# Delta-net stage: a head's four input projections as two pairs of seven half-size products

## The chip, the cores and the metric

The kernel runs on one core of one Trainium2 chip. The core has a matrix engine (TensorE, PE in the profile, with its weight loads as PEld), a vector engine (VectorE, DVE), a scalar engine (ScalarE, ACT), a general engine (GpSimd, POOL), and DMA queues, here issued by SyncE (SPq) and ScalarE (ACTq). They run side by side and wait for each other by semaphores. The metric is the device time of one execution in microseconds (us).

## The reference

Two blocks of a residual network on a 512 x 1024 activation, all float32. The change touches one mixer of the first block, a gated delta-net with 8 heads of width 128:

```python
proj = h @ w_in
qkv, z, a, bt = jnp.split(proj, [n_qkv, n_qkv + H * dv, n_qkv + H * dv + H], axis=-1)
qkv = jax.nn.silu(causal_dwconv(qkv, conv_w))          # 4 taps along the sequence
q, k, v = jnp.split(qkv, [H * dk, 2 * H * dk], axis=-1)
q = _l2norm(_chunk_heads(q, H, C)) * (dk ** -0.5)
k = _l2norm(_chunk_heads(k, H, C))
...                                                     # beta, g, decays from a and bt
sol = lax.linalg.triangular_solve(kk + eye, rhs, left_side=True, lower=True, unit_diagonal=True)
u, w = sol[..., :dv], sol[..., dv:]
...                                                     # a scan over chunks makes o
o = o * lax.rsqrt(jnp.mean(o * o, axis=-1, keepdims=True) + 1e-6) * norm_w
o = o * jax.nn.silu(z)                                  # gate
return o.reshape(b_, s, H * dv) @ w_out
```

Per head there are four projections of the same input h (512 x 1024): q, k, v and z, each by 1024 x 128 weights.

## The kernel before

Everything is kept transposed: `HT` (128 x 8 x 512) holds the input, features on partitions. The weights come through `ring`, three slots of 2 MB; one slot holds a head's four units q, k, v, z (128 x 8 x 128 each). Between the heads' loads stand those of `ada` (weights of a conditioning vector), which VectorE sums in place (`dve_ada`, L387); a slot's next load is issued when its last reader is done.

A unit is 8 matmuls of 128 x 128 weights against 512 columns into one bank (`pe_dense4`, L1264). In float32 every matmul is two records in the trace. VectorE reads the bank with four convolution taps (`dve_conv4`: L1622 the first, L1625 three more), ScalarE applies SiLU (`silu`, L1522); the fourth unit, z, goes through `gate` (L1550) to the one buffer `zs`.

A head is an iteration h of a loop with two parts. First six levels of a blockwise triangular inverse. In each level TensorE makes `LD` (L1396), VectorE masks it (`Tm`, L1747), TensorE makes `TE` (L1414), VectorE subtracts (`inv`, L1753), TensorE transposes (`DT`, L1422), VectorE copies (`D`, L1768), and the next `LD` waits for that. Between these TensorE fills in the projections of head h+1: `fill` places 2, 1 and 1 matmuls behind LD, TE and DT. Then comes the scan over four chunks (L1434 to L1460), with 8 matmuls of head h+2 (`ahead`) between its steps, and the start of the next head's chain on VectorE: `lower` (L1683), `d_first` (L1696, L1699), `e_first` (L1704, L1706), the end of `dve_ada`, `gated` (L1717), `inner` (L1712). GpSimd has three products per head: two masks (`decay`, L1829 and L1832) and the scaled query (`qe`, L1838). All orders are written out by hand; each engine runs its list in order.

`khat` (L1671) and `qhat` (L1676) scale key and query, `kk` (L1318) is the first product of the next head. The final head fills with matmuls of the output projection (`gdn_ahead`) instead. The feed-forward stages (`pe_up`, L537) already use seven products of half size, with 256 columns each.

## Time and profile before

| | us |
|---|---|
| median of 3 runs | 2706.67 |
| lowest and highest | 2705.37, 2707.93 |
| the profiled execution's own time | 2705.38 |
| its span from first to last instruction | 2703.6 |

Between the span and the profiled execution's time lie 1.8 us outside the instructions. The delta-net stage reaches from about 43 us to about 520 us of the span.

### The profile page before, as it was taken

What the parts mean: (1) busy time and instruction counts of PE and PEld (TensorE: products, weight loads), DVE (VectorE), ACT (ScalarE), POOL (GpSimd) and SP (SyncE); (2) the same over time, 40 slices, a digit from 0 to 9 for tenths busy, and PEclk for the clock granted to TensorE, in tenths of its full rate; (3) what the DMA queues carried; (4) which work ended last, traced back from release to release, by engine and by line L of the source; (5) the groups of instructions that cost most, each with busy time, mean ns of one, the idle gap of its engine ahead of it and who ended that gap; (6) DMA issues with size and microseconds to landing.
All of it is one profiled execution on the core that took longest, in us unless ns stands there. A gap on an engine that the chain in (4) does not pass through costs nothing.

```text
span 2703.6 us, 30522 instructions
## 1 busy us (share of the span) xinstructions
PE 2611.0 (97%) x11992; PEld 1963.3 (73%) x11992; DVE 1650.5 (61%) x2935; ACT 682.9 (25%) x1293; POOL 146.1 (5%) x114
## 2 busy tenths in 40 slices
PE   7999999999999999999999999998999998999999
PEld 2566666568888877888887888885445454888888
DVE  2666667487776454554647877654465486766652
ACT  2334343131111021112102111003443364222200
POOL 0000010010000020000001000001121000000000
PEclk9999999999999999999999999999999999999999
DMA  8121122135443321121122544331021310122121
GB/s 351 63 94 63 63 75 91 54 125 187 159 154 146 117 98 70 67 98 67 63 80 81 190 155 180 143 122 67 31 80 63 125 63 32 63 94 94 60 91 53
DMA packets 25357, 275.02 MB, mean 102 GB/s; under 512 B 3576, under 2 KB 4472, under 8 KB 8192
## 3 DMA queue, kind: packets, MB, share of 16 engines
q1 hardware_dynamic: 21760, 268.39, 26.6%
q10 hardware_dynamic: 3456, 4.69, 0.5%
q8 instruction: 96, 1.57, 0.2%
q14 instruction: 45, 0.37, 0.0%
HBM read 270.97 MB, written 2.10 MB: 101 GB/s over the span
## 4 chain that ended last, share of the span: by engine, by line
PE 90%; DVE 5%; ACT 2%; DMA 1%; issue 1%; POOL 0%; SPq 0%; DVEq 0%; ACTq 0%; POOLq 0%
PE bank L537 29%; PE bank L619 14%; PE bank L2150 10%; PE bank L1264 8%; PE bank L2551 4%; PE bank L412 4%; PE bank L1937 4%; PE bank L1396 2%; PE bank L1414 2%; PE bank L2235 1%; DMA arena<-w_ada 1%; PE bank L2544 1%; PE bank L2999 1%; PE bank L1422 1%; PE bank L2683 1%
## 5 line engine op out<-in xcount | busy, mean ns | idle before, releaser
L537 PE MATMUL bank<-HT,ring 128*128 128x256 f32 x1056 | 252.4, 386 | 9.8 <-ACT HT L945 7.4
L1264 PE MATMUL bank<-HT,ring 128*128 128x512 f32 x512 | 250.3, 597 | 5.6 <-ACT arena L1550 5.6
L537 PE MATMUL bank<-arena,ring 128*128 128x256 f32 x1056 | 249.5, 379 | 0.0
L537 PE MATMUL bank<-arena 128*128 128x256 f32 x1056 | 249.5, 379 | 0.0
L537 PEld LDWEIGHTS bank<-HT,ring 128*128 128x128 f32 x1056 | 202.5, 193 | 45.2 <-issue 15.5
L537 PEld LDWEIGHTS bank<-arena,ring 128*128 128x128 f32 x1056 | 200.6, 190 | 27.3
L537 PEld LDWEIGHTS bank<-arena 128*128 128x128 f32 x1056 | 200.6, 190 | 27.3
L619 PE MATMUL bank<-arena,ring 128*128 128x256 f32 x936 | 207.3, 380 | 9.4 <-ACT arena L691 5.6
L619 PEld LDWEIGHTS bank<-arena,ring 128*128 128x128 f32 x936 | 177.0, 190 | 37.0 <-ACT arena L691 6.8
L1185 ACT ACTIVATE arena<-bank,ffc 128x512 f32<-128x512 f32 x66 | 51.3, 778 | 486.7 <-DVE bank L1093 486.7
L2551 PE MATMUL bank<-HT,ring 128*128 128x512 f32 x320 | 148.2, 604 | 3.0 <-ACT HT L985 3.0
L537 PE MATMUL bank<-HT,arena 128*128 128x256 f32 x528 | 125.5, 380 | 1.7 <-DVE arena L1150 1.6
L1264 PEld LDWEIGHTS bank<-HT,ring 128*128 128x128 f32 x512 | 84.0, 191 | 58.0 <-issue 57.1
L619 PE MATMUL bank<-arena 128*128 128x256 f32 x528 | 116.4, 379 | 0.0
L537 PEld LDWEIGHTS bank<-HT,arena 128*128 128x128 f32 x528 | 99.6, 190 | 17.7 <-DVE arena L1150 4.5
L2150 PE MATMUL bank<-arena,ring 128*128 128x256 f32 x512 | 112.4, 379 | 0.0
L619 PEld LDWEIGHTS bank<-arena 128*128 128x128 f32 x528 | 100.3, 190 | 13.6
L2150 PEld LDWEIGHTS bank<-arena,ring 128*128 128x128 f32 x512 | 97.2, 190 | 14.7 <-issue 1.4
L972 POOL TENSOR_SCALAR XT<-XT,comb_v 128x512 f32<-128x512 f32 x32 | 49.2, 1549 | 1077.2 <-ACT HT L945 674.4
L387 DVE SCALAR_TENSOR_TENSOR arena<-ring,evec,arena 128x512 f32<-128x512 f32 x140 | 104.7, 748 | 2.6
L2551 PEld LDWEIGHTS bank<-HT,ring 128*128 128x128 f32 x320 | 57.8, 192 | 63.1 <-issue 57.5
L1103 DVE SCALAR_TENSOR_TENSOR arena<-bank,ffc,arena 128x511 f32<-128x511 f32 (+1 forms) x132 | 98.5, 746 | 2.9 <-ACT arena L1185 0.6
(470 smaller groups left out, 4216.7 us busy)
## 6 DMA issues: line engine op xcount, KB each, us to landing
ring<-w_ada SPq DMA_DIRECT2D x33, 2048.0 KB, 8.2
ring<-w_up SPq DMA_DIRECT2D x33, 2048.0 KB, 7.6
ring<-w_down SPq DMA_DIRECT2D x24, 1408.0 KB, 6.1
ring<-w_gdn SPq DMA_DIRECT2D x7, 2048.0 KB, 8.7
ring<-w_ret_qk SPq DMA_DIRECT2D x4, 2048.0 KB, 7.7
ring<-w_ret_v SPq DMA_DIRECT2D x4, 2048.0 KB, 7.6
ring<-w_ret_g SPq DMA_DIRECT2D x4, 2048.0 KB, 7.7
ring<-w_ret_out SPq DMA_DIRECT2D x4, 2048.0 KB, 7.6
```

Of the source, the lines that this page charges most:

```text
L387: ins = nc.vector.scalar_tensor_tensor(out=acc, in0=w[:, :, k, :], scalar=evec[:, e, k:k + 1], in1=acc, op0=ALU.mult, op1=ALU.add)
L412: ins = nc.tensor.matmul(B[bank][:, :], out_weights(pe, tag, n, k), src(k), start=(first and k == k0), stop=(last and k == k1 - 1))
L537: last = nc.tensor.matmul(out_, w[:, k, :], x[:, k, :], start=(first and k == 0), stop=(k == 3), skip_group_check=not first)
L619: last = nc.tensor.matmul(out_, w[:, k, :], x(k), start=(first and k == 0), stop=(k == KH2 - 1), skip_group_check=not first)
L1103: last = nc.vector.scalar_tensor_tensor(out=out_[:, m:], in0=src[:, 0:T - m], scalar=ffc[:, i, j, half, 2 - m:3 - m], in1=out_[:, m:], op0 ...
L1185: nc.scalar.activation(ffn_y[:, j % 2, :], up_bank(j)[:, :], ACT.Identity, scale=ffc[:, i, j, 0, 2:3], bias=ffc[:, i, j, 0, 3:4])\
L1264: last = nc.tensor.matmul(B[u % 2][:, :], w[:, u, k, :], HT[:, k, :], start=(k == 0), stop=(k == KC - 1))
L1396: last = nc.tensor.matmul(B4[5][:, i, :], G["LT4"][:, i, :], G["D4"][:, i, :], start=True, stop=True)
L1414: last = nc.tensor.matmul(B4[4][:, i, :], G["Tm4"][:, i, :], G["E4"][:, i, :], start=True, stop=True)
L1937: last = nc.tensor.matmul(out_, w[:, k, :], x[:, k, :], start=(first and fresh and k == 0), stop=(k == 7), skip_group_check=not (first and ...
L2150: last = nc.tensor.matmul(out_, left, right, start=flag, stop=(k == 3), skip_group_check=not (first and fresh))
L2551: last = nc.tensor.matmul(bank[:, :], w[:, u, k, :], HT[:, k, :], start=(k == 0), stop=(k == KC - 1))
```

## The change

A pair of units (a, b) times the input is a product of 2 x 2 blocks: the weights' halves over the features are A11, A12 (unit a) and A21, A22 (unit b), the input's quarters are HT's two halves of features and two halves of columns. The change computes the 2 x 2 product with seven products instead of eight (M1 to M7), each 4 matmuls against 256 columns. The pairs are (q, k) and (z, v): 56 matmuls of 256 columns per head instead of 32 of 512.

- **Input sums.** `gdn_T`, four arrays of 128 x 4 x 256, are made once by VectorE before the first head.
- **Weight sums.** GpSimd makes four per pair (S3, S2, S1, S4), each 128 x 512, in place in the ring's slot (`third`, `others`): S2, S1 and S4 overwrite weights that M7, M1 and M2 have read. Eight more GpSimd operations per head.
- **Output sums.** ScalarE copies M1 and M7 (and for q one finished quarter, c11) out of the banks, three copies for pair 0 and two for pair 1. VectorE adds t, U2, c21, c22, c12 per pair, each on 256 columns. q, k and v now end in memory (`gdn_raw`) instead of a bank; z stays in its bank.
- **Taps.** ScalarE makes the first tap (`tap`), VectorE three (`dve_taps`); these read the projection from SBUF instead of PSUM.
- **Order.** `fill` places 3, 2, 2 of the new matmuls per level, `ahead` 14 in the steps of `GDN_AHEAD`. The v taps move to levels 1 and 2 of their own head, `vtok` from level 2 to 3, `gcb` from level 3 to 4. `khat` moves from ahead of `inv` in level 6 to behind it. `gate` moves from the end of an iteration to before the scan, and has two buffers. In `act_gdn` `silu` of key comes before that of query.
- **Tables.** `sel` is no longer loaded; its product is read from `ident`, and its memory holds v and the second z buffer; `wab` holds k.

```diff
...
+assert o <= 19968
+raw_q = region(19968, T)
+raw_k = wab[:, :, :].rearrange("p k n -> p (k n)")
+raw_v = sel[:, 0:4, :].rearrange("p i c -> p (i c)")
+gdn_raw = (raw_q, raw_k, raw_v)
+zs = [G["zs"], sel[:, 4:8, :].rearrange("p i c -> p (i c)")]
...
+GDN_UNITS = ((0, 1), (3, 2))
+GDN_ORDER = ("M1", "M7", "M2", "M4", "M5", "M6", "M3")
+PAIR = 28
+GDN_AHEAD = (0, 2, 4, 6, 8, 10, 12, 13, 14)
+def gdn_quarters(h, p):
+    w = ring[:, load_at[("gdn", h)] % SLOTS, :].rearrange("p (u k n) -> p u k n", u=4, k=KC)
+    u0, u1 = GDN_UNITS[p]
+    return w[:, u0, 0:4, :], w[:, u0, 4:8, :], w[:, u1, 0:4, :], w[:, u1, 4:8, :]
+def pair_before(h, p):
+    return (h, 0) if p else (h - 1, 1)
...
+def pe_steps(pe, h, s0, s1):
+    for s in range(s0, s1):
+        p, name, k = s // PAIR, GDN_ORDER[s % PAIR // 4], s % 4
+        A11, A12, A21, A22 = gdn_quarters(h, p)
+        Bg, Bx = B[p], B[1 - p]
+        if name == "M1":
+            out_, w, x, first = Bg[:, 0:TH], A11, HT[:, 0:4, 0:TH], True
+            if k == 0:
...
+                if h or p:
+                    pe.wait_ge(dve_done, at("dve", "gdn", "c21", *pair_before(h, p)))
+        elif name == "M7":
+            out_, w, x, first = Bx[:, 0:TH], A21, gdn_T[2], True
+            if k == 0:
...
+                if p:
+                    pe.wait_ge(dve_done, at("dve", "gdn", "c12", h, 0))
+                elif h:
+                    pe.wait_ge(act_done, at("act", "gdn", "z", h - 1))
+                pe.wait_ge(pool_done, at("pool", "gdn", "S3", h, p))
+        elif name == "M2":
+            out_, w, x, first = Bg[:, 0:TH], A12, HT[:, 4:8, 0:TH], False
+            if k == 0:
+                pe.wait_ge(act_done, at("act", "gdn", "m1", h, p))
+        elif name == "M4":
...
+        elif name == "M5":
+            out_, w, x, first = Bg[:, TH:T], A11, gdn_T[0], True
+            if k == 0:
+                pe.wait_ge(pool_done, at("pool", "gdn", "S1", h, p))
+                if p == 0:
+                    pe.wait_ge(act_done, at("act", "gdn", "c11", h))
+        elif name == "M6":
+            out_, w, x, first = Bx[:, TH:T], A21, gdn_T[1], True
+            if k == 0:
+                pe.wait_ge(pool_done, at("pool", "gdn", "S2", h, p))
+        else:
+            out_, w, x, first = Bg[:, TH:T], A12, HT[:, 4:8, TH:T], False
+            if k == 0:
+                pe.wait_ge(pool_done, at("pool", "gdn", "S4", h, p))
+                pe.wait_ge(dve_done, at("dve", "gdn", "t", h, p))
+        last = nc.tensor.matmul(out_, w[:, k, :], x[:, k, :], start=(first and k == 0), stop=(k == 3), skip_group_check=not first)
+        if k == 3:
+            last.then_inc(pe_done, PE.tick("gdn", name, h, p))
...
-        def fill(n0, n1):
+        def fill(l, n0, n1):
             if more:
-                pe_dense4(pe, ("gdn", h + 1), 8 + n0, 8 + n1)
+                s = GDN_AHEAD[-1] + 7 * (l - 1)
+                pe_steps(pe, h + 1, s + (0, 3, 5, 7)[n0], s + (0, 3, 5, 7)[n1])
             else:
...
         def ahead(n0, n1):
             if h + 2 < GH:
-                pe_dense4(pe, ("gdn", h + 2), n0, n1)
+                pe_steps(pe, h + 2, GDN_AHEAD[n0], GDN_AHEAD[n1])
...
-            if l == 2:
+            if l == 3:
                 vtok(h)
-            if l == 3 and more:
+            if l == 4 and more:
                 gcb(h + 1)
-            fill(4 * l - 4, 4 * l - 2)
+            fill(l, 0, 1)
...
+    def keep_m1(h, p):
+        act.wait_ge(pe_done, at("pe", "gdn", "M1", h, p))
+        if h or p:
+            act.wait_ge(dve_done, at("dve", "gdn", "U2", *pair_before(h, p)))
+        nc.scalar.activation(gdn_m1, B[p][:, 0:TH], ACT.Copy).then_inc(act_done, AC.tick("gdn", "m1", h, p))
...
+    def tap(h, u):
+        act.wait_ge(dve_done, at("dve", "gdn", *(("c12", h, 0), ("c22", h, 0), ("c22", h, 1))[u]))
...
+        nc.scalar.activation(G[("cq", "ck", "cv")[u]], gdn_raw[u], ACT.Copy, scale=gconv[:, u * GH + h, 3:4])\
+            .then_inc(act_done, AC.tick("gdn", "tap", h, u))
...
-        act.wait_ge(pe_done, at("pe", "gdn", "proj", h, 3))
-        if h:
-            act.wait_ge(dve_done, at("dve", "gdn", "gated", h - 1))
-        nc.scalar.activation(G["zs"], B[1][:, :], ACT.Silu).then_inc(act_done, AC.tick("gdn", "z", h))
+        act.wait_ge(dve_done, at("dve", "gdn", "c12", h, 1))
+        if h >= 2:
+            act.wait_ge(dve_done, at("dve", "gdn", "gated", h - 2))
+        nc.scalar.activation(zs[h % 2], B[1][:, :], ACT.Silu).then_inc(act_done, AC.tick("gdn", "z", h))
...
+def dve_taps(dve, h, u, j0, j1):
+    out_, src = G[("cq", "ck", "cv")[u]], gdn_raw[u]
     for j in range(j0, j1):
-        tap = gconv[:, u * GH + h, 3 - j:4 - j]
-        if j == 0:
-            ins = nc.vector.tensor_scalar(out_, src[:, :], tap, None, ALU.mult)
+        if j == 1:
+            dve.wait_ge(act_done, at("act", "gdn", "tap", h, u))
         else:
             dve.wait_ge(dve_done, conv_step[0])
-            ins = nc.vector.scalar_tensor_tensor(out=out_[:, j:], in0=src[:, 0:T - j], scalar=tap, in1=out_[:, j:],
-                                                 op0=ALU.mult, op1=ALU.add)
-        ins.then_inc(dve_done, DV.tick("gdn", "conv", h, u))
+        nc.vector.scalar_tensor_tensor(out=out_[:, j:], in0=src[:, 0:T - j], scalar=gconv[:, u * GH + h, 3 - j:4 - j], in1=out_[:, j:],
+                                       op0=ALU.mult, op1=ALU.add).then_inc(dve_done, DV.tick("gdn", "conv", h, u))
         conv_step[0] = DV.n
+def dve_pair(dve, h, p):
+    Bg, Bx = B[p], B[1 - p]
+    def t():
+        dve.wait_ge(pe_done, at("pe", "gdn", "M5", h, p))
+        dve.wait_ge(act_done, at("act", "gdn", "m7", h, p))
+        dve.wait_ge(dve_done, DV.n)
+        nc.vector.tensor_tensor(gdn_t, Bg[:, TH:T], gdn_m7, ALU.add).then_inc(dve_done, DV.tick("gdn", "t", h, p))
+    def U2():
+        dve.wait_ge(pe_done, at("pe", "gdn", "M6", h, p))
+        dve.wait_ge(act_done, at("act", "gdn", "m1", h, p))
+        dve.wait_ge(dve_done, DV.n)
+        nc.vector.tensor_tensor(gdn_U2, Bx[:, TH:T], gdn_m1, ALU.add).then_inc(dve_done, DV.tick("gdn", "U2", h, p))
+    def c21():
+        dve.wait_ge(pe_done, at("pe", "gdn", "M4", h, p))
+        dve.wait_ge(dve_done, DV.n)
+        nc.vector.tensor_tensor(gdn_raw[1 + p][:, 0:TH], Bx[:, 0:TH], gdn_U2, ALU.add).then_inc(dve_done, DV.tick("gdn", "c21", h, p))
...
+    return t, U2, c21, c22, c12
...
             if more:
-                if l < 5:
-                    dve_conv4(dve, h + 1, (l - 1) // 2, 2 * ((l - 1) % 2), 2 * ((l - 1) % 2) + 1)
+                if l == 1:
+                    dve_taps(dve, h, 2, 1, 2)
+                elif l == 2:
+                    ta[1]()
+                    dve_taps(dve, h, 2, 3, 4)
+                elif l == 3:
+                    ta[4]()
+                elif l == 4:
+                    dve_taps(dve, h + 1, 1, 3, 4)
                 elif l == 5:
-                    dve_conv4(dve, h + 1, 2, 0, 1)
+                    dve_taps(dve, h + 1, 0, 3, 4)
                 else:
-                    dve_conv4(dve, h + 1, 2, 3, 4)
-                    khat(h + 1)
+                    tb[0]()
                 inverse()
                 if l <= NT:
                     tokens(l - 1)
                 if l < 6:
                     dve.wait_ge(pe_done, at("pe", "gdn", "DT", h, l))
                     nc.vector.tensor_copy(G["D"], B[6][:, :]).then_inc(dve_done, DV.tick("gdn", "D", h, l))
-                if l == 2 and h:
+                if l == 1:
+                    dve_taps(dve, h, 2, 2, 3)
+                    ta[0]()
+                elif l == 2:
+                    ta[2]()
+                    ta[3]()
+                elif l == 3:
+                    dve_taps(dve, h + 1, 1, 1, 3)
+                elif l == 4:
+                    dve_taps(dve, h + 1, 0, 1, 3)
+                elif l == 5 and h:
                     normed(h - 1)
-                if l < 5:
-                    dve_conv4(dve, h + 1, (l - 1) // 2, 2 * ((l - 1) % 2) + 1, 2 * ((l - 1) % 2) + 2)
-                elif l == 5:
-                    dve_conv4(dve, h + 1, 2, 1, 3)
-                else:
+                elif l == 6:
+                    tb[1]()
+                    tb[2]()
+                    khat(h + 1)
+                    tb[3]()
+                    tb[4]()
                     qhat(h + 1)
...
+    def third(h, p):
+        A11, A12, A21, A22 = gdn_quarters(h, p)
...
+        if h or p:
+            n = load_at[("gdn", h)]
+            pool.wait_ge(ring_full[n % SLOTS], landed(n))
+        nc.gpsimd.tensor_tensor(A21, A11, A21, ALU.subtract).then_inc(pool_done, PO.tick("gdn", "S3", h, p))
+    def others(h, p):
+        A11, A12, A21, A22 = gdn_quarters(h, p)
+        pool.wait_ge(pe_done, at("pe", "gdn", "M7", h, p))
+        pool.wait_ge(pool_done, at("pool", "gdn", "S3", h, p))
+        nc.gpsimd.tensor_tensor(A21, A22, A21, ALU.subtract).then_inc(pool_done, PO.tick("gdn", "S2", h, p))
+        pool.wait_ge(pool_done, at("pool", "gdn", "S2", h, p))
+        pool.wait_ge(pe_done, at("pe", "gdn", "M1", h, p))
+        nc.gpsimd.tensor_tensor(A11, A11, A21, ALU.add).then_inc(pool_done, PO.tick("gdn", "S1", h, p))
+        pool.wait_ge(pe_done, at("pe", "gdn", "M2", h, p))
+        nc.gpsimd.tensor_tensor(A12, A12, A21, ALU.subtract).then_inc(pool_done, PO.tick("gdn", "S4", h, p))
...
+    for h in range(GH - 1):
+        third(h + 1, 1)
+        if h + 2 < GH:
+            third(h + 2, 0)
+        others(h + 1, 1)
+        decay(h + 1)
+        if h + 2 < GH:
+            others(h + 2, 0)
+        query(h + 1)
...
```

Three places in the orders. TensorE before, level 2 of an inner head (L1396 LD, L1354 vtok, L1264 fill, L1414 TE, L1422 DT):

```order
L1396 MATMUL bank<-arena 128x128 x4
L1354 MATMUL bank<-ident,arena 128x128 x4
L1264 MATMUL bank<-HT,ring 128x512 x2
L1414 MATMUL bank<-arena 128x128 x4
L1264 MATMUL bank<-HT,ring 128x512
L1422 MATMUL bank<-ident,arena 128x128 x4
L1264 MATMUL bank<-HT,ring 128x512
```

and now, the same level, where L1453 is LD, L1315 the fill, L1471 TE, L1479 DT:

```order
L1453 MATMUL bank<-arena 128x128 x4
L1315 MATMUL bank<-arena,ring 128x256 x3
L1471 MATMUL bank<-arena 128x128 x4
L1315 MATMUL bank<-HT,ring 128x256 x2
L1479 MATMUL bank<-ident,arena 128x128 x4
L1315 MATMUL bank<-HT,ring 128x256 x2
```

Two, one and one matmuls of 512 columns became three, two and two of 256, and vtok went one level on.

VectorE before, from Tm of level 1 to Tm of level 2 and the work up to inv:

```order
L1747 TENSOR_TENSOR arena<-bank,maskL 128x512
L384 TENSOR_SCALAR arena<-ring,evec 128x512
L1622 TENSOR_SCALAR arena<-bank,gconv 128x512
L1753 TENSOR_TENSOR arena<-arena,bank 128x512
L1741 TENSOR_SCALAR arena<-bank,arena 128x128
L1742 TENSOR_SCALAR arena<-bank,arena 128x128
L1768 COPY arena<-bank 128x512
L1625 SCALAR_TENSOR_TENSOR arena<-bank,gconv,arena 128x511
L1747 TENSOR_TENSOR arena<-bank,maskL 128x512
L387 SCALAR_TENSOR_TENSOR arena<-ring,evec,arena 128x512
L1625 SCALAR_TENSOR_TENSOR arena<-bank,gconv,arena 128x510
L1753 TENSOR_TENSOR arena<-arena,bank 128x512
```

and now from D of level 1 to inv of level 2 (L1935 D, L1730 a tap, L1743 t, L1908 Tm, L1750 U2, L1914 inv):

```order
L1935 COPY arena<-bank 128x512
L1730 SCALAR_TENSOR_TENSOR arena<-sel,gconv,arena 128x510
L1743 TENSOR_TENSOR HT<-bank,HT 128x256
L1908 TENSOR_TENSOR arena<-bank,maskL 128x512
L387 SCALAR_TENSOR_TENSOR arena<-ring,evec,arena 128x512
L1750 TENSOR_TENSOR HT<-bank,HT 128x256
L1730 SCALAR_TENSOR_TENSOR arena<-sel,gconv,arena 128x509
L1914 TENSOR_TENSOR arena<-arena,bank 128x512
```

A tap read a bank and now reads `sel`; t stands ahead of Tm and U2 ahead of inv.

GpSimd before, one head:

```order
L1829 TENSOR_TENSOR arena<-arena,causal 128x512
L1832 TENSOR_TENSOR arena<-arena,causal 128x512
L1838 TENSOR_TENSOR arena<-arena 128x512
```

and now (L2017 S3, L2024 S2, L2027 S1, L2029 S4, L2035 and L2038 the masks, L2047 the query):

```order
L2017 TENSOR_TENSOR ring<-ring 128x512 x2
L2024 TENSOR_TENSOR ring<-ring 128x512
L2027 TENSOR_TENSOR ring<-ring 128x512
L2029 TENSOR_TENSOR ring<-ring 128x512
L2035 TENSOR_TENSOR arena<-arena,causal 128x512
L2038 TENSOR_TENSOR arena<-arena,causal 128x512
L2024 TENSOR_TENSOR ring<-ring 128x512
L2027 TENSOR_TENSOR ring<-ring 128x512
L2029 TENSOR_TENSOR ring<-ring 128x512
L2047 TENSOR_TENSOR arena<-arena 128x512
```

Eight sums joined the three products, three of them between the masks and the query.

## Rows read from the trace of the kernel before

**Rows 1.** The page's first part: busy time, share of the span, instructions of each engine.

```profile
PE 2611.0 (97%) x11992; PEld 1963.3 (73%) x11992; DVE 1650.5 (61%) x2935; ACT 682.9 (25%) x1293; POOL 146.1 (5%) x114
```

**Rows 2.** Windows, one head: busy us, instructions, granted clock, DMA share, GB/s.

```profile
249.86:305.24 55.38, 54.44 (x268) 34.28 (x268) 37.26 (x65) 20.95 (x37) 4.24 (x3) 1.00 0.21 76
```

**Rows 3.** Groups by form, delta-net stage: busy us, mean ns, idle before.

```profile
L1264 PE MATMUL bank<-HT,ring 128*128 128x512 f32 x512 | 250.3, 597 | 5.6 <-ACT arena L1550 5.6
L1625 DVE SCALAR_TENSOR_TENSOR arena<-bank,gconv,arena 128x511 f32<-128x511 f32 x24 | 17.8, 742 | 0.1
```

**Rows 4.** Timeline, level 5 of an inner head: start us, us, engine, idle before.

```profile
278.02 1.16 PE L1396 MATMUL bank<-arena 128*128 128x128 f32 x8
...
279.02 1.88 PE L1264 MATMUL bank<-HT,ring 128*128 128x512 f32 x4
279.22 0.69 DVE L1747 TENSOR_TENSOR arena<-bank,maskL 128x512 f32<-128x512 f32 x1 [0.59 <-PE bank L1396]
...
280.74 1.05 PE L1414 MATMUL bank<-arena 128*128 128x128 f32 x8
...
281.63 1.02 PE L1264 MATMUL bank<-HT,ring 128*128 128x512 f32 x2
281.83 0.69 DVE L1753 TENSOR_TENSOR arena<-arena,bank 128x512 f32<-128x512 f32 x1 [0.60 <-PE bank L1414]
...
282.57 0.66 PE L1422 MATMUL bank<-ident,arena 128*128 128x128 f32 x4
...
283.26 0.69 DVE L1768 COPY arena<-bank 128x512 f32<-128x512 f32 x1 [0.75 <-PE bank L1422]
```

**Rows 5.** Timeline, feed-forward stage: two runs of eight records, a 256-column addition.

```profile
600.44 1.89 PE L537 MATMUL bank<-arena 128*128 128x256 f32 x8
...
602.16 1.93 PE L537 MATMUL bank<-HT,arena 128*128 128x256 f32 x8
602.55 0.42 DVE L1161 TENSOR_TENSOR arena<-bank,wab 128x256 f32<-128x256 f32 x1
```

**Rows 6.** Timeline, end of level 6: GpSimd's masks beside VectorE's khat, qhat.

```profile
288.17 1.28 POOL L1829 TENSOR_TENSOR arena<-arena,causal 128x512 f32<-128x512 f32 x1 [39.05 <-ACT arena L1511]
...
288.65 1.34 DVE L1671 TENSOR_TENSOR arena<-arena 128x512 f32<-128x512 f32 x1
...
289.40 1.73 POOL L1832 TENSOR_TENSOR arena<-arena,causal 128x512 f32<-128x512 f32 x1
...
289.92 0.68 DVE L1753 TENSOR_TENSOR arena<-arena,bank 128x512 f32<-128x512 f32 x1
...
290.86 1.05 PE L1434 MATMUL bank<-arena 128*128 128x128 f32 x8
```

**Rows 7.** One line's instructions: least, median, most ns.

```profile
L2782 DVE SCALAR_TENSOR_TENSOR arena<-arena x16: 676/690/1760, 1899.4 to 2066.4; 128x512 f32<-128x512 f32 x16
```

**Rows 8.** Timeline, from one head to the next.

```profile
303.36 1.69 DVE L1706 TENSOR_TENSOR arena<-ident,arena 128x512 f32<-128x512 f32 x1
...
305.07 1.05 PE L1396 MATMUL bank<-arena 128*128 128x128 f32 x8
...
306.52 0.33 SPq L3308 DMA_DIRECT2D ring<-w_gdn  x1
...
307.61 0.68 DVE L1747 TENSOR_TENSOR arena<-bank,maskL 128x512 f32<-128x512 f32 x1
...
307.93 1.96 PE L1264 MATMUL bank<-HT,ring 128*128 128x512 f32 x4 [0.94 <-ACT arena L1550]
...
309.72 1.05 PE L1414 MATMUL bank<-arena 128*128 128x128 f32 x8
```

**Rows 9.** DMA issues in the stage: count, size, us from issue to landing.

```profile
ring<-w_gdn SPq DMA_DIRECT2D x6, 2048.0 KB, 8.6
```

**Rows 10.** One line's instructions: input sums of 1024 elements, feed-forward stage.

```profile
L1080 DVE TENSOR_TENSOR arena<-HT x3: 1225/1634/1682, 569.1 to 2302.9; 128x1024 f32<-128x1024 f32 x3
```

**Rows 11.** Timeline, start of the stage: ScalarE's first exponentials of the decay rows.

```profile
53.58 0.63 ACT L1490 ACTIVATE arena<-arena 8x512 f32<-8x512 f32 x1 [3.28 <-DVE arena L1653]
```

189 lines of the change are left out of this document (125 added, 64 removed).

## Prediction

> **What bounds the kernel now.** I read the page's engine shares first: TensorE is busy for 97% of the span, GpSimd for 5% [rows 1]. So TensorE sets the end, if its work is dense where the change acts. Then the delta-net stage by windows: one head takes 55.38 us at full granted clock, 54.44 of it TensorE, 37.26 VectorE, 20.95 ScalarE, 4.24 GpSimd [rows 2]. The projections are 64 records in a head, 512 over 8 heads [rows 3]. Four of them, from 279.02 to the next matmul at 280.74, take 1.72 us, so a full 512-column matmul (two records) costs 0.86 us and the 32 of a head 27.5 us.
>
> The stage is not free of waits, and the timeline of one level tells which [rows 4]. LD starts at 278.02, its result goes to Tm at 279.22 (1.20 later). TE starts at 280.74, 2.72 after LD. inv starts 1.09 after TE, at 281.83, DT 0.74 after inv, D 0.69 after DT, and the next LD can start 0.75 after D. From TE on, this chain through VectorE is as long as TensorE's own: TE 0.89 and one fill of 0.86 make 1.75, inv's path 1.09 + 0.74 makes 1.83. So TE to DT and DT to LD are a tie that VectorE wins by 0.08. Only between LD and TE has TensorE the longer road: LD 1.00 and two fills 1.72, where Tm would let TE go at 1.20 + 0.75 = 1.95. VectorE's idle time before Tm is 0.59, before inv 0.60 [rows 4]. These are what the change may spend.
>
> **TensorE's part.** Seven 256-column products: from 600.44 to 602.16 eight records of 256 columns take 1.72 us, 0.215 each [rows 5]; a matmul costs 0.43, half of 0.86. 56 x 0.43 = 24.1 us instead of 27.5: 3.4 us less per head, 27 us over eight, if TensorE is never made to wait. That isn't the gain, since the saved steps must fall where TensorE is the longer road. Fill two and three of a level hold 2 x 0.43 = 0.86, as before: nothing. The first holds 1.29 instead of 1.72: 0.43 per level, and TE then starts at 2.29, still behind 1.95. Six levels less in seven iterations (the last fills with other work). In the scan the pieces are 0.86 as before but for the last two, 0.43 each; the saving there only brings LD forward, from 305.07 to 304.2.
>
> **From head to head.** There TE of level 1 starts at 309.72, 4.65 after LD at 305.07 [rows 8]. The fill before it starts at 307.93, held 0.94 by gate; the change gives gate a second buffer and an earlier place, so this wait goes. Next late is VectorE: Tm starts at 307.61, so TE could go at 308.36. The possible gain is 1.36 per head in six boundaries.
>
> **VectorE's part.** Per head it loses three first taps (0.74 each, like the others in [rows 3]) and gets ten 256-column sums of 0.42 [rows 5], at a spacing near 0.35: about 1.3 us more in a head where it is busy 37.26 of 55.38. Placed level by level: t behind a tap after D, 1.0 us where D's end to Tm leaves 1.3; c21 and c22 0.7; two taps in levels 3 and 4, 1.3, just full. Before inv: U2 and a tap in level 2, 1.0 instead of 0.66, where the earlier TE has cut the idle 0.60 to 0.17, so inv is 0.1 to 0.2 late; levels 1, 3, 4, 5 have one tap or less and are in time. khat's move takes it off inv's path, but U starts at 290.86 when fill two and three end [rows 6], so that gives nothing beyond the 0.43. Levels 2 to 6, before contention: 5 x 0.43 less 0.2, that is -1.9 us per head. ScalarE's five copies and three taps, about 4 us, lie in idle time of an engine that is busy 38% of a head.
>
> **GpSimd's part.** Eight sums of 1.28 us (the length of its product in [rows 6]) per head: 10.2 us more, to 14.5 of 54. TensorE has M7's wait for S3, M5's for S1, M6's for S2, M3's for S4; there are 8 matmuls (3.4 us plus the levels' own work) between M7's end and M5, for 2.6 us of GpSimd, so in steady state these are met. In [rows 6] lies the cost. GpSimd's mask starts at 288.17 and ends at 289.45; VectorE's khat, issued at 288.65, ends at 289.99 and takes 1.34 instead of some 0.69; GpSimd's next takes 1.73 instead of 1.28. inv, which reads a bank, runs beside it in 0.68. A three-operand form with both inputs in SBUF shows the same: 0.69 at the median, 1.76 at the most [rows 7]. So one VectorE operation with two SBUF inputs that meets a GpSimd product waits up to 1.07 us, and the two take turns. The taps become such operations, from bank to SBUF; ada's steps are already.
>
> The Trainium skill states this as a rule ("SBUF — State Buffer", section "SBUF: two separate sides"): VectorE with two SBUF inputs and GpSimd reading SBUF take one shared pair of ports as a lock for the whole instruction, and the loser blocks. The trace agrees, by 1.34 against 0.69 us. It speaks against this change; my sum has such waits in (a) to (c), and if the engines shared freely the absorbed case below would stand.
>
> Where they meet, from the positions above. (a) Scan's end: M7 of head h+2 ends near 298.5 on the scale of [rows 8], so S2, S1 run to 301.6, S4 to 303.2, the query to 304.9, S3 after it. d_first's two steps and e_first wait in turn; vn of the last chunk comes 0.7 later, which costs what the shorter ahead saves there; the second e_first step (303.36, 1.69 long) was hit by the query before as well, and ends about 0.4 later; one ada step waits 1.1 behind S3. Tm thus starts near 309.0 instead of 307.61 and TE at 309.75: the 1.36 of the gate is eaten, +0.1 per head. (b) Level 2: S3 of the next head waits for its weights, whose load is issued behind ada (306.52, now near 307.9) and lands 8.6 us later [rows 9], 2.8 us after LD of level 2, just when the level's tap is issued (2.9). If the sum is first, inv is 1.1 late; if the tap is first, nothing. I take half, +0.6. (c) Level 4: S2 starts at 2.9 behind the tap, S1 and S4 fill the time to LD of level 5; the two taps behind D wait 0.4, of which the slack takes most. Zero, at most 1 us.
>
> **Start and end of the stage.** At the start VectorE makes four sums of 1024 elements, 1.23 us each [rows 10], two of them ahead of the memsets from which the decay rows' chain runs. These rows reach their exponentials at 53.58 [rows 11], now near 57.5 to 58.5; ScalarE's nine DMA issues stand behind them and M2 of pair 1 waits for the copy behind those. TensorE's saving there, 3.4 us, is spent: kk of head 0 comes about 1 us later, the first LD 1.5 to 2.5. I take +2.5, between -1 (all hidden) and +5. In the last head three taps in one level: +0.9.
>
> **The sum.** Levels 7 x -1.9 = -13.3; level 2's meeting 7 x 0.6 = +4.2; boundaries 6 x 0.1 = +0.6; start +2.5; last head +0.9. Together -5.1 us. On the profiled execution's 2705.38 (1.8 outside the span) that is 2700.3; this execution is 1.3 below the median 2706.67, so on the median 2701.6. (c) and (b) both rest on coincidences of 0.1 us, and of the two I hold (b) for a little likelier to fall well, since the tap needs nothing from outside: I say 2701.
>
> **The rivals.** *Contention absorbed* (chance 0.2). If the sums fall beside operations on banks, which [rows 6] shows unhurt, levels give -13.3, boundaries 6 x -1.36 = -8.2, start and end +1: -20.5, 2686. For it: VectorE has 18 us of idle time in a head. Against: two-input operations stand at nearly every place.
>
> *GpSimd and VectorE in turns* (0.2, slower). In levels 3 to 5 every tap and ada step that meets S2, S1 or S4 goes behind it, and with no slack after the shorter fill each passes straight to inv or Tm. With three such meetings per head beyond my sum, 0.65 us each behind what slack takes: 7 x 1.95 = +13.7, 2715. It decides from 0.8 us per head, where my gain of 5.7 is gone. For it: [rows 6] shows two in a row already with two GpSimd products; now there are three.
>
> *The chain through VectorE gives nothing back* (0.15). If t, U2 or c12 wait for their product and delay Tm and inv by 0.3 per level, the levels' 0.43 is gone; with start and end the time is 2706 to 2708, no change.
>
> **How the numbers follow.** The likeliest (0.45) reaches from 2694 to 2705 by the bounds of start, (b) and (c). It lies below 2701.3 in some 0.3 and above in 0.15. A measurement of this kernel can tell about 0.2%, 5.4 us. Faster: 0.2 + 0.3 = 0.5. Within: 0.15 + 0.15 = 0.3. Slower: 0.2. The range takes in the absorbed case's centre and most of the slower one: 2685 to 2713.
>
> **What would show it.** L1315's records 0.215 us apart; TE 2.3 us after LD in levels 2 to 6; level 5 about 5.6 long instead of 5.99; taps (L1730) with a most well over 0.75, ada steps too; VectorE's e_first near 1.7; TE of level 1 some 5.3 after LD; a head of about 54.1 us or less. Waits of L1315 for GpSimd would prove me wrong, and so would a median tap of 1.3 us.

## The result: slower by half a per cent

The changed kernel takes 2722.03 us (median of 4 runs, 2719.35 to 2722.77), the kernel before beside it 2706.56: a ratio of 1.0053, 95% interval 1.0041 to 1.0064. The forecast was 2701 with a range of 2685 to 2713; the time moved the other way, by 15 us. The profiled execution of the changed kernel took 2722.39 us with a span of 2720.4, so what its trace shows is the median case. Lines of the changed kernel are other numbers: LD of a level is L1453, TE L1471, a projection product L1315, Tm L1908, inv L1914, a tap L1730, GpSimd's sums are L2017 (S3), L2024, L2027, L2029 (S2, S1, S4).

The page of the changed kernel, its first part, to be held against [rows 1]:

```profile
PE 2608.1 (96%) x12376; PEld 2051.0 (75%) x12376; DVE 1692.4 (62%) x2995; ACT 713.5 (26%) x1358; POOL 237.4 (9%) x178
```

TensorE has 12.5% fewer projection columns in the stage and yet its busy time falls by only 2.9 us. Two windows tell why. The columns are as in [rows 2]: the stretch, its length, busy time of PE, PEld, DVE, ACT, POOL, granted clock, DMA share, GB/s. The first two rows are two heads, from LD of level 1 to the next head's; the next two are the beginning of the first of them, cut where the granted clock falls.

```profile
200.75:257.76 57.01, 54.69 (x316) 46.16 (x315) 41.16 (x72) 24.75 (x46) 16.01 (x12) 0.94 0.20 74
257.76:312.68 54.92, 51.53 (x315) 43.32 (x314) 42.20 (x72) 24.73 (x46) 15.68 (x12) 1.00 0.21 77
200.75:207.50 6.75, 4.63 (x30) 3.64 (x28) 6.52 (x9) 3.52 (x4) 2.15 (x2) 1.00 0.33 102
207.50:214.40 6.90, 6.90 (x26) 6.08 (x27) 2.77 (x6) 0.00 (x0) 1.57 (x1) 0.51 0.48 204
```

An inner head took 55.38 us before. Here one takes 54.92, at full granted clock, and its neighbour 57.01, with 6.9 us in which the clock was granted at half (0.51, the level of 1.2 GHz instead of 2.4). The timeline of TensorE shows what stands just ahead of that stretch; the columns are those of [rows 4].

```profile
202.51 1.46 PE L1315 MATMUL bank<-arena,ring 128*128 128x256 f32 x6
206.09 1.16 PE L1471 MATMUL bank<-arena 128*128 128x128 f32 x8 [2.12 <-DVE arena L1908]
207.09 1.33 PE L249 MATMUL bank<-ones,arena 128*128 128x1 f32 x8
208.28 2.05 PE L1315 MATMUL bank<-arena,ring 128*128 128x256 f32 x4
```

TE of level 1 waits 2.12 us for Tm, and the four records of L1315 behind it take 2.05 us instead of 1.03. In the heads of the changed kernel the granted clock falls so at 94.9, 149.5, 207.5, 320.1 and 374.7, each time 0.4 to 2.1 us behind the end of this wait, for 3.4 or 6.8 us; in two heads with the same wait it doesn't fall, and behind a wait of 2.27 at 58.0, at the start of the stage, it doesn't either. So such a wait is often followed by half the clock, not always. The kernel before waits at most 0.94 in an inner head and has no such stretch between the one at 29.6 and the one at 521 us. Why Tm is late is in the timeline of VectorE and GpSimd in the head at 257.76, the place of [rows 8]:

```profile
256.50 1.72 POOL L2047 TENSOR_TENSOR arena<-arena 128x512 f32<-128x512 f32 x1
257.13 1.64 DVE L1866 TENSOR_TENSOR arena<-ident,arena 128x512 f32<-128x512 f32 x1
258.18 1.71 POOL L2017 TENSOR_TENSOR ring<-ring 128x512 f32<-128x512 f32 x1
258.69 2.54 DVE L387 SCALAR_TENSOR_TENSOR arena<-ring,evec,arena 128x512 f32<-128x512 f32 x2
262.35 0.68 DVE L1908 TENSOR_TENSOR arena<-bank,maskL 128x512 f32<-128x512 f32 x1
263.09 1.16 PE L1471 MATMUL bank<-arena 128*128 128x128 f32 x8 [2.12 <-DVE arena L1908]
```

The two ada steps take 2.54 instead of 1.50 beside S3, e_first's second step 1.64 behind the query's product. TE starts 5.33 after LD (257.76 to 263.09), where the prediction says "some 5.3" (its own positions in (a), 304.2 and 309.75, give 5.55). What it lacked is what TensorE's clock does behind such a wait.

**Where the 16.8 us are.** Each instruction of TensorE in one trace, held against the same one of the other counted from the end, gives the offset at every point: +3.7 at LD of level 1 of head 0 (86.27 before, 89.95 after), +8.3 at that of head 7 (467.0, 475.3), +8.7 at the end of the stage near 510 us, and then, where no line of code differs, +10.2 at 530, +12.5 at 990, +14.1 at 1455, +16.9 at 1922, +16.8 at the end. In this pair of traces half of the loss lies outside the code that was changed. The split is not fixed: `x9_after_pos` below has the same stage, and its trace stands at +12.4 at the end of the stage and at +13.5 at the end.

### The profile page after: what moved, and what is told of

The parts are those of the page before. It is cut to its first block, busy times and chain, and to the rows that moved or that the text cites. A ratio compares the mean times of both kernels' runs of the same rounds, so it can differ in the third digit from the quotient of the medians.

```text
span 2720.4 us, 31649 instructions
## 1 busy us (share of the span) xinstructions
PE 2608.1 (96%) x12376; PEld 2051.0 (75%) x12376; DVE 1692.4 (62%) x2995; ACT 713.5 (26%) x1358; POOL 237.4 (9%) x178
## 3 DMA queue, kind: packets, MB, share of 16 engines
q8 instruction: 100, 1.64, 0.2%
## 4 chain that ended last, share of the span: by engine, by line
PE 86%; DVE 8%; ACT 2%; DMA 2%; issue 1%; POOL 0%; SPq 0%; DVEq 0%; ACTq 0%; POOLq 0%
PE bank L537 28%; PE bank L619 14%; PE bank L2377 10%; PE bank L1315 6%; PE bank L2778 4%; PE bank L412 4%; PE bank L2164 4%; PE bank L1453 1%; PE bank L1471 1%; PE bank L2462 1%; DMA arena<-w_ada 1%; PE bank L2771 1%; DVE arena L387 1%; PE bank L1479 1%; PE bank L3226 1%
## 5 line engine op out<-in xcount | busy, mean ns | idle before, releaser
L537 PE MATMUL bank<-HT,ring 128*128 128x256 f32 x1056 | 252.6, 386 | 9.8 <-ACT HT L945 7.4
L537 PE MATMUL bank<-arena,ring 128*128 128x256 f32 x1056 | 249.5, 379 | 0.0
L537 PEld LDWEIGHTS bank<-HT,ring 128*128 128x128 f32 x1056 | 202.5, 193 | 45.4 <-issue 15.5
L537 PEld LDWEIGHTS bank<-arena,ring 128*128 128x128 f32 x1056 | 200.7, 190 | 27.2
L619 PE MATMUL bank<-arena,ring 128*128 128x256 f32 x936 | 207.3, 380 | 9.6 <-ACT arena L691 5.6
L619 PEld LDWEIGHTS bank<-arena,ring 128*128 128x128 f32 x936 | 177.1, 190 | 37.3 <-ACT arena L691 6.8
L2778 PE MATMUL bank<-HT,ring 128*128 128x512 f32 x320 | 149.9, 609 | 3.0 <-ACT HT L985 3.0
L1315 PE MATMUL bank<-arena,ring 128*128 128x256 f32 x512 | 138.8, 400 | 1.2 <-DVE arena L1788 0.8
L387 DVE SCALAR_TENSOR_TENSOR arena<-ring,evec,arena 128x512 f32<-128x512 f32 x140 | 111.8, 798 | 2.6
L2377 PE MATMUL bank<-arena,ring 128*128 128x256 f32 x512 | 112.5, 379 | 0.0
L1315 PEld LDWEIGHTS bank<-arena,ring 128*128 128x128 f32 x512 | 94.2, 200 | 20.0 <-issue 8.2
L2377 PEld LDWEIGHTS bank<-arena,ring 128*128 128x128 f32 x512 | 97.2, 190 | 14.8 <-issue 1.4
L2778 PEld LDWEIGHTS bank<-HT,ring 128*128 128x128 f32 x320 | 58.5, 194 | 64.1 <-issue 58.6
L1315 PE MATMUL bank<-HT,ring 128*128 128x256 f32 x384 | 97.1, 382 | 3.4 <-DVE HT L1743 2.3
```

What stands on the lines that cost most here:

```text
L387: ins = nc.vector.scalar_tensor_tensor(out=acc, in0=w[:, :, k, :], scalar=evec[:, e, k:k + 1], in1=acc, op0=ALU.mult, op1=ALU.add)
L537: last = nc.tensor.matmul(out_, w[:, k, :], x[:, k, :], start=(first and k == 0), stop=(k == 3), skip_group_check=not first)
L619: last = nc.tensor.matmul(out_, w[:, k, :], x(k), start=(first and k == 0), stop=(k == KH2 - 1), skip_group_check=not first)
L1315: last = nc.tensor.matmul(out_, w[:, k, :], x[:, k, :], start=(first and k == 0), stop=(k == 3), skip_group_check=not first)
L2377: last = nc.tensor.matmul(out_, left, right, start=flag, stop=(k == 3), skip_group_check=not (first and fresh))
L2778: last = nc.tensor.matmul(bank[:, :], w[:, u, k, :], HT[:, k, :], start=(k == 0), stop=(k == KC - 1))
```

## Experiments

All ratios are to the kernel before on the same chip; beside the four groups of runs it took 2706.56, 2706.88 (x1 to x4), 2705.68 (x5 to x8) and 2706.28 us (x9 to x11). Four questions: does the fallen clock cost what it seems to (x1), do GpSimd's sums alone make the wait (x2, x3, and x4 for the gate), can they stand elsewhere (x5, x6), and what is the loss outside the stage (x7 to x11).

### Keep TensorE busy in the wait

```diff
                     fill(l, 0, 1)
+                    if l == 1:
+                        for n in range(5):
+                            nc.tensor.matmul(B[7][:, TH:T], ident[:, :], HT[:, n, 0:TH], start=True, stop=True, skip_group_check=True)
                     pe.wait_ge(dve_done, at("dve", "gdn", "Tm", h, l))
```

> The changed kernel with five matmuls of 256 columns (2.15 us by the pitch of 0.43) that feed nothing, into an unused half of bank 7, put ahead of TE's wait in level 1 of every head, where TensorE waited 2.1 us for VectorE's Tm. Clock theory (the wait at the head's start lets the granted clock fall; the heads with a 6.8 us spell at half clock took 57.0 us, those without 53.8 to 54.9): the five spells inside the stage go, heads are all near 54, the time is 2709 to 2715 instead of 2722. Rival (the wait itself is the loss, the spells cost nothing on top): 2722, within 2.

Measured: 2712.76 us (10 runs), ratio 1.0022, interval 1.0012 to 1.0031. TensorE in an inner head, and the window of this head:

```profile
253.74 1.46 PE L1315 MATMUL bank<-arena,ring 128*128 128x256 f32 x6
255.04 2.32 PE L1464 MATMUL bank<-HT,ident 128*128 128x256 f32 x10
257.32 0.94 PE L1474 MATMUL bank<-arena 128*128 128x128 f32 x6
251.99:306.74 54.75, 53.65 (x325) 45.22 (x324) 42.04 (x72) 24.76 (x46) 15.71 (x12) 1.00 0.21 78
```

TE follows LD by 5.33 (251.99 to 257.32) exactly as without the five products, so these bring nothing forward. They only fill the wait, and no stretch at half clock is left in the heads. Some 9 us are back, by work of no use. In the heads alone, from LD of level 1 of head 0 to that of head 7, it is 376.6 against 385.35 us. That the fallen clock costs about 9 us here is shown, and that it needs TensorE's pause: Tm ends as late as in the changed kernel, and only the pause is filled. That it doesn't follow from the pause alone is in the two heads above.

### Without the sums, and the sums alone

The changed kernel without `third` and `others`, and without TensorE's four waits for them (in head 0 it waits for the weights' loads instead; the weights' halves are then multiplied as they lie, so the projections are others):

```diff
-                        pe.wait_ge(pool_done, at("pool", "gdn", "S3", h, p))
...
-                third(h + 1, 1)
-                if h + 2 < GH:
-                    third(h + 2, 0)
-                others(h + 1, 1)
```

> The changed kernel with GpSimd's weight sums left out, and TensorE's waits for them, so its projections are not the reference's. Contention theory (VectorE's two-input operations wait behind GpSimd): Tm of level 1 starts 1.4 us or more earlier, a head takes about 52 us, no spell at half clock, 2684 to 2692. Rival (the loss is in the output sums on VectorE and the copies on ScalarE, which stay): not below 2700.

Measured: 2698.06 (4 runs), ratio 0.9962, interval 0.9947 to 0.9977. And the kernel before with eight GpSimd subtractions of the same size per head, into a region of no use, at about the points at which the changed kernel has its sums:

```diff
+            def extra(n):
+                pool.wait_ge(pool_done, PO.n)
+                nc.gpsimd.tensor_tensor(scratch[n], HT[:, 0, :], HT[:, 1, :], ALU.subtract).then_inc(pool_done, PO.tick())
```

> The kernel before with eight GpSimd subtractions per head (two inputs from SBUF, 128 x 512, into unused memory) released at about the places of the change's sums; nothing else changed, the output stays the reference's. Contention theory: d_first, e_first and ada steps take up to 1.7 us each, Tm of level 1 starts later than the gate's wait, TE waits for it; 2712 to 2722, with spells at half clock in the stage. Rival (GpSimd's share is harmless and the rest of the change costs): 2706.5, within 3.

Measured: 2724.36, ratio 1.0061, interval 1.0044 to 1.0078: 17.5 us slower than before, with nothing else changed. TE of level 1 in the first, and the waits in level 1 of the second:

```profile
247.25 0.94 PE L1473 MATMUL bank<-arena 128*128 128x128 f32 x6 [0.88 <-DVE arena L1910]
243.17:295.54 52.37, 51.29 (x316) 43.48 (x315) 38.25 (x72) 24.75 (x46) 4.17 (x4) 1.00 0.22 81
```

```profile
256.73 2.54 DVE L387 SCALAR_TENSOR_TENSOR arena<-ring,evec,arena 128x512 f32<-128x512 f32 x2
260.71 1.95 PE L1264 MATMUL bank<-HT,ring 128*128 128x512 f32 x4 [2.45 <-ACT arena L1550]
```

Without sums TE starts 4.08 after LD, a head is 52.37 long, VectorE is busy 38.25 of it instead of 42.20: GpSimd's eight sums cost VectorE 3.95 us a head. With the sums alone the gate waits behind the same slowed steps, 2.45 instead of the 0.94 of [rows 8], and TE starts 6.1 to 7.8 after LD, with a stretch at half clock in three heads. So VectorE's and GpSimd's turns are the origin of the longer wait, in either kernel; 0.88 us of it is there without the sums too. The second run came 2.4 us above the 2712 to 2722 that were expected. The first was expected at 2684 to 2692 and missed that by 6 us: its heads gave what was expected (17.0 us less than before at the stage's end), but 9 us were given back outside.

### The gate alone

The kernel before with the second buffer and the earlier place of `gate`, as in the change:

```diff
...
-                if h:
-                    act.wait_ge(dve_done, at("dve", "gdn", "gated", h - 1))
-                nc.scalar.activation(G["zs"], B[1][:, :], ACT.Silu).then_inc(act_done, AC.tick("gdn", "z", h))
+                if h >= 2:
+                    act.wait_ge(dve_done, at("dve", "gdn", "gated", h - 2))
+                nc.scalar.activation(zs[h % 2], B[1][:, :], ACT.Silu).then_inc(act_done, AC.tick("gdn", "z", h))
...
                 if more:
+                    gate(h + 1)
                     silu(h + 1, 2)
...
-                if more:
-                    gate(h + 1)
...
```

> The kernel before with the gate alone changed: two z buffers, and gate of the next head ahead of the scan (ScalarE, in front of silu of v) instead of behind it. By my sum's step on the boundary TE of level 1 starts 1.36 us earlier in six heads: 2698.4, between 2697 and 2700. Rival (another wait there ends last, such as Tm's at the same time): 2706.5, within 2.

Measured: 2699.25 (6 runs), ratio 0.9969, interval 0.9957 to 0.998.

```profile
248.71 1.88 PE L1265 MATMUL bank<-HT,ring 128*128 128x512 f32 x4
250.43 0.83 PE L1415 MATMUL bank<-arena 128*128 128x128 f32 x6
246.96:301.16 54.20, 54.20 (x267) 34.36 (x266) 37.24 (x65) 20.82 (x38) 4.24 (x3) 1.00 0.21 78
```

The boundary gives 1.17 us per head (TE 3.47 after LD instead of 4.65), where the prediction had 1.36 at most, and TensorE is busy for the whole of the head (54.20 of 54.20). This small part of the change is a gain of 7 us by itself; the sums took it away again.

### The sums in other windows

The changed kernel, with S3 of the pair (z, v) of the next head (`third(h + 1, 1)`) held until inv of level 1 is done, and S3 of the pair (q, k) of the head after it (`third(h + 2, 0)`) until inv of level 2 is done, and with each what stands behind it in GpSimd's order. (The expectation names the units otherwise; this is what the edit does.)

```diff
+                pool.wait_ge(dve_done, at("dve", "gdn", "inv", h, 1))
                 third(h + 1, 1)
                 if h + 2 < GH:
+                    pool.wait_ge(dve_done, at("dve", "gdn", "inv", h, 2))
                     third(h + 2, 0)
```

> The changed kernel with GpSimd's sums of a head moved: the key's second unit waits for VectorE's inv of level 1, the two sums of the value's unit for inv of level 2, so that levels 1 and 2 have no sum beside them except what is due. Contention-then-clock theory (the sums beside level 1 make VectorE late, TensorE waits 2.1 us at TE of level 1, and its granted clock falls to half behind that wait): TE follows LD of level 1 by 4.1 to 4.7 us as in the run without the sums (4.08), no half-clock spell in the heads, a head 52.6 to 53.6 us (without the sums 52.37), 9 to 13 us less than before at the stage's end, and 2694 to 2704 us in all, since spells outside the stage may take up to 8 us back as they did there. Rival (the sums cost the same wherever they stand, since the dearer levels 3 and 4 then bear them): the time is moved and not saved, a head stays at 54.5 us or more and the whole at 2710 or more.

Measured: 2702.13 (10 runs), ratio 0.998, interval 0.9969 to 0.9991. Level 1 of an inner head, and the head:

```profile
252.36 1.52 DVE L387 SCALAR_TENSOR_TENSOR arena<-ring,evec,arena 128x512 f32<-128x512 f32 x2
255.74 1.16 PE L1471 MATMUL bank<-arena 128*128 128x128 f32 x8 [1.10 <-DVE arena L1908]
257.70 1.27 POOL L2017 TENSOR_TENSOR ring<-ring 128x512 f32<-128x512 f32 x1 [5.81 <-DVE arena L1914]
251.42:304.25 52.83, 51.53 (x315) 43.32 (x314) 40.12 (x72) 24.75 (x46) 15.29 (x12) 1.00 0.22 80
```

Two waits on GpSimd, which is idle most of the time, turn 20 us. From LD of level 1 of head 0 to that of head 7 it is 368.7 instead of 385.35 us: TE is 1.0 earlier in six heads (6.1), less is lost at half clock (8.2), and level 2 is 5.75 or 5.85 long in every head (2.2). The ada steps are back at 1.52, S3 takes 1.27 instead of 1.71 beside operations that read a bank, TensorE's wait is 1.10, the granted clock stays full in heads 2 to 6 (it still falls in head 0, where the first TE waits 2.09, and once in head 1), and a head is 52.83 instead of 54.92 to 57.01. The rival (moved, not saved) is out. Two parts of the expectation were missed: the clock does fall in two heads, and the stage's end is 7.3 us earlier than before in the trace instead of 9 to 13.

At the start of the stage the changed kernel shows one more meeting. This is VectorE's scaling of XT there, in one group, and the exponentials of [rows 11] behind it:

```profile
50.16 5.98 DVE L1790 TENSOR_SCALAR XT<-XT 128x512 f32<-128x512 f32 x8
59.86 0.63 ACT L1582 ACTIVATE arena<-arena 8x512 f32<-8x512 f32 x1 [7.02 <-DVE arena L1804]
```

The eight scalings take 5.98 us (2.8 in the kernel before), and ahead of them stand the input sums; the rows come 6.3 us later than before. `x6_windows_xt` takes the kernel above and moves the scalings behind the prologue's chain, ahead of `khat(0)`:

```diff
-            for n in range(KC):
-                nc.vector.tensor_scalar(XT[:, n, :], XT[:, n, :], ALPHA, None, ALU.mult).then_inc(dve_done, DV.tick())
...
+            for n in range(KC):
+                nc.vector.tensor_scalar(XT[:, n, :], XT[:, n, :], ALPHA, None, ALU.mult).then_inc(dve_done, DV.tick())
             khat(0)
```

> The kernel of x5_windows with VectorE's eight scalings of XT (0.75 us each beside GpSimd's sums in the changed kernel, 0.35 each before) moved from the head of its prologue chain to the place just ahead of the first head's khat. If those scalings stood on the path that sets the start of head 0, its LD of level 1 comes 2 to 3 us earlier than 89.95, and the whole is 2 to 3 us below x5_windows (2691 to 2702). Rival (the first head's start hangs on the chain of projections and taps, and the scalings move into it at its end): within 1 us of x5_windows, or later by up to 3 us where they stand ahead of khat.

Measured: 2699.82 (10 runs), ratio 0.9977, interval 0.9968 to 0.9987; LD of level 1 of head 0 at 87.47 instead of 90.57 in `x5_windows`. That is 3.1 us at the start in these two traces, but `x5_windows` has a stretch at half clock at 58.7 us there and this trace has none, so a part of it can be the clock. In a later trace of the same start (`x10_windows_xt_pos`), with such a stretch at 65.2 us, this LD is at 89.4, 1.2 earlier. The medians of the whole differ by 2.3, but the single runs spread over 5.5 us (`x5_windows`) and 9.4 us (`x6_windows_xt`) and the two intervals overlap. The LD comes 2.5 us earlier than the 89.95 of the changed kernel, as expected; that the move is worth 2 us of the whole is not shown.

### What is lost outside the stage

First the plainest idea: that a shift of the program alone moves stretches at half clock to other places. The kernel before with useless products at the very end of TensorE's part of the stage, 22 and 11 of them:

```diff
             osum(GH - 1)
+            for n in range(22):
+                nc.tensor.matmul(B[5][:, 0:TH], ident[:, :], HT[:, n % KC, 0:TH], start=True, stop=True, skip_group_check=True)
             pe_ada(pe, 0, 3 + GH)
```

> The kernel before with 22 products of 256 columns of no use at the very end of TensorE's part of the stage (each 0.11 us at the full granted clock, no result read): only the position of all that follows is moved, by 2.4 us of TensorE's own work, or by what it takes at half the clock. Theory that the 7.5 us which the changed kernel loses outside the stage come from half-clock spells that fall on other stretches when the program is shifted: the delay at the end differs from that at the stage's end by more than 2 us, with other spells in the records, so the whole is above 2711 or at 2707 or below. Rival (code outside the stage takes a fixed time): the delay of the stage's end and the delay at the end agree within 1 us, 2709 us.

> The same with 11 such products (1.2 us of TensorE's work). Shifted-spells theory: the delay at the end is not half of that of x7_delay22 but differs by several us in either direction, with spells at other places than before. Rival (fixed time): half of that delay within 1 us, 2708 us.

Measured: 2716.07 (5 runs; ratio 1.0034, interval 1.0021 to 1.0047) and 2710.1 (10 runs; 1.0022, 1.0012 to 1.0031), against 2705.68 before: +10.4 and +4.4 by the medians, 9.2 and 6.0 by the ratios. One number in these expectations is mine and wrong, the length of a product. The trace of the first (22 products, 44 records, partly at half clock, where the previous wait is 1.26):

```profile
518.49 2.07 PE L1360 MATMUL bank<-arena,ones 128*128 128x512 f32 x2 [1.26 <-ACT arena L1608]
520.36 10.45 PE L1469 MATMUL bank<-HT,ident 128*128 128x256 f32 x44
```

A product is 0.43 us by [rows 5], so 22 are 9.4 and 11 are 4.7. The delays of the medians are these within 1.0 and 0.3 us, and both intervals hold them. The stretches at half clock do move (one near 850 us that the kernel before doesn't have; the one at 1880 gone), and the offset steps by 2.3 us between 571 and 990, but over the rest of the program it comes out nearly even. A mere shift is worth about 1 us in the medians and about 2 in the two traces (from 530 us to the end the offset goes from 8.7 to 10.7 and from 2.5 to 4.4), not 7.5. That idea fell as the whole cause.

The offset's largest step outside the stage is the one between 1455 and 1922 us, 2.7. All five kernels with the changed stage measured so far have a step of 2.7 us or more there, none with the stage of before has one over 0.3. VectorE and TensorE at that place, in the kernel before:

```profile
1885.80 0.43 DVE L2624 CAST arena<-arena 128x512 f32<-128x512 int32 x1 [1.54 <-DMA arena<-in_pos]
...
1902.03 0.43 PE L2676 MATMUL bank<-arena,comb 128*32 128x128 f32 x8 [1.05 <-POOL arena L2830]
1902.38 3.70 PE L2551 MATMUL bank<-HT,ring 128*128 128x512 f32 x8
```

and in the changed one:

```profile
1900.99 0.43 DVE L2851 CAST arena<-arena 128x512 f32<-128x512 int32 x1 [2.49 <-DMA arena<-in_pos]
...
1917.21 0.43 PE L2903 MATMUL bank<-arena,comb 128*32 128x128 f32 x8 [1.99 <-POOL arena L3057]
1917.56 5.38 PE L2778 MATMUL bank<-HT,ring 128*128 128x512 f32 x8
```

The same load, issued at the same place in ScalarE's program, lands 3.6 us after its issue instead of 2.6 (the load in the kernel before, then in the changed one):

```profile
L2585 ACTq DMA_DIRECT2D arena<-in_pos x1: 334/334/334, 1883.1 to 1883.1; - x1
DMA to landing us min/median/max: 2.6/2.6/2.6
```

```profile
L2812 ACTq DMA_DIRECT2D arena<-in_pos x1: 335/335/335, 1897.3 to 1897.3; - x1
DMA to landing us min/median/max: 3.6/3.6/3.6
```

VectorE waits 0.95 longer, through GpSimd TensorE does too (1.99 instead of 1.05), and behind that longer pause the granted clock falls for 3.4 us, so that eight records take 5.38 instead of 3.70. 0.94 + 1.68 = 2.6 us. The test issues this load some 9 us earlier, ahead of the norm:

```diff
         def act_mix_front(act, units_out):
...
-            act.dma_start(angle[0].bitcast(I32), dr["pos"]).then_inc(nsa_tables_in, 16)
...
+            act.dma_start(angle[0].bitcast(I32), dr["pos"]).then_inc(nsa_tables_in, 16)
             act_rms(act, "norm4", "norm4")
```

in the changed kernel, in `x6_windows_xt`, and in the kernel before as the control.

> The changed kernel with one load outside the stage issued earlier: in_pos (256 KB, issued by ScalarE at 1897.3, landing 3.6 us later, 2.6 in the kernel before), which VectorE waits for 2.49 us (1.54 before) and TensorE behind it 1.99 us (1.05 before), with half the clock for 3.4 us behind that wait, which the kernel before does not have. It is issued ahead of the norm, some 9 us earlier. Theory (2.7 of the 7.5 us that the changed kernel loses outside the stage come from this landing and the clock that falls behind it): TensorE's wait for the comb task of 1.99 us is at most 1.0, no half-clock spell follows, the offset to the kernel before no longer steps from 14.2 to 16.9 at 1902, and the whole is 2717.5 to 2720. Rival (the step is something else of the changed program, and another releaser takes the place of the load): the wait stays above 1.5 us and the whole at 2722.

> x6_windows_xt with the same load issued earlier. Theory: 2.5 to 3.7 us below it, 2696 to 2697.5, the fastest of all. Rival: 2699 to 2700 as x6_windows_xt.

> The kernel before with the same load issued earlier, as the control: it has no half-clock spell behind this wait, so only the wait of 1.05 us can go. Theory: 2704.5 to 2706, 0 to 1.1 us below before. Rival (the early load is worth the same to both programs): 2702 to 2703.

Measured, against 2706.28 before: 2718.14 (ratio 1.0042, interval 1.0027 to 1.0057), 2696.8 (0.9964, 0.9953 to 0.9976) and 2706.31 (1.0, 0.9991 to 1.001). Above the time before, the changed kernel was 15.5 us and is 11.9; `x6_windows_xt` was 5.9 below and is 9.5 below; before is where it was. So in the medians the early load is worth 3.6 us where the changed stage stands ahead of it and nothing where it doesn't, about as the theory said. The intervals of each pair overlap, so one pair alone wouldn't show it; both pairs give the same, and the traces show the place. The control is 0.3 us above what was expected of it. In the trace of `x10_windows_xt_pos` TensorE's wait at this place is down to 1.23 us and no stretch at half clock follows; in that of `x9_after_pos` neither engine waits at this place and TensorE goes on at full rate:

```profile
1913.79 0.43 PE L2902 MATMUL bank<-arena,comb 128*32 128x128 f32 x8
1914.15 3.70 PE L2778 MATMUL bank<-HT,ring 128*128 128x512 f32 x8
```

Between 1455 and 1922 us the offset falls by 0.9 in the first trace and by 1.1 in that of the control, and it rises by 1.0 in that of `x10_windows_xt_pos`, where it rose by 2.8, 0.0 and 2.9 with the load at its old place. So the control's wait does go too, about 1 us at this place. Its trace has a new stretch at half clock at 2174 us that takes 1.4 back, and `x9_after_pos` has two new ones, at 2186 and 2585 us, that take 1.7.

Why the load lands 1 us later is argued, not shown. It is the same 144 packets; the last starts 3.14 us behind the issue instead of 2.31. In the five traces with the changed stage and the load at its old place two packets with instructions, of the queue q14, fall between issue and landing (8 KB each, 1.6 and 2.1 us behind the issue in the changed kernel), and the landing takes 3.5 to 3.7 us; in the four with the old stage and one such packet it takes 2.6 to 2.7; in `x8_delay11`, with one of them and one of 16 KB of the queue q8, 3.2; in the three with the early load there is none, and it takes 2.5 to 2.6 in either program. The remaining steps outside the stage (about 1.5 at 530, 2.0 before 990, 1.7 at 1033 us) are at stretches at half clock that are longer than before or that before hasn't; in `x9_after_pos` these are absent, but its stage, with the same code, took 3.7 us more than that of the changed kernel. They differ from trace to trace, and what decides them stays open.

`x10_windows_xt_pos` is faster than both kernels, by 9.5 us against before. It is not clearly ahead of `x4_before_gate`, which changes about ten lines of the kernel before (intervals 0.9953 to 0.9976 and 0.9957 to 0.998).

## The prediction, step by step

From positions of LD and TE in the two traces, over the seven heads, in us against before:

| step | predicted | measured |
|---|---|---|
| levels 2 to 5, seven heads | -10.3 | -9.8 |
| level 6, and the boundary to TE of level 1 (a) | -3.0 + 0.6 | -1.8 |
| from there to LD of level 2, six heads | 0 | +0.7 |
| level 2 meets S3 of the next head (b) | +4.2 | +2.2 |
| first head's level 1 | not in the sum | +2.7 |
| start of the stage | +2.5 | +3.7 |
| last head | +0.9 | +0.4 |
| clock granted at half in the heads | not in the sum | +10.5 |
| outside the stage | not in the sum | +8.1 |
| together | -5.1 | +16.7 (offset at the end 16.8) |

**TensorE's part and levels 2 to 6 were right.** Level 2 is 0.57 us shorter where S3 doesn't meet it (6.42 to 5.85), levels 3 and 4 together 0.41 (13.22 to 12.81; `gcb` has moved from one to the other), level 5 0.41 (7.62 to 7.21). The "5.6 instead of 5.99" for level 5 was misread: 5.99 is level 4's. GpSimd's sums in level 4 cost nothing that counts, (c): `x2_no_sums` has 6.00, 6.81 and 7.20 without them. The changed kernel shows the turns there that slack absorbs, two taps at 1.68 instead of 1.53:

```profile
285.90 1.27 POOL L2029 TENSOR_TENSOR ring<-ring 128x512 f32<-128x512 f32 x1
286.21 0.69 DVE L1935 COPY arena<-bank 128x512 f32<-128x512 f32 x1 [0.23 <-PE bank L1479]
286.82 1.68 DVE L1730 SCALAR_TENSOR_TENSOR arena<-arena,gconv 128x511 f32<-128x511 f32 x2
286.96 1.16 PE L1453 MATMUL bank<-arena 128*128 128x128 f32 x8
```

**The contention was sized right in (a), on the balance in (b).** TE of level 1 stands 5.33 after LD, where the forecast said some 5.3 and its positions 5.55. In (b) the sum or an ada step comes first, by where the load lands:

```profile
269.03 1.26 POOL L2017 TENSOR_TENSOR ring<-ring 128x512 f32<-128x512 f32 x1 [9.13 <-DMA ring<-w_gdn]
269.03 1.81 DVE L387 SCALAR_TENSOR_TENSOR arena<-ring,evec,arena 128x512 f32<-128x512 f32 x1
272.71 0.66 PE L1479 MATMUL bank<-ident,arena 128*128 128x128 f32 x4 [1.27 <-DVE arena L1914]
```

That head's level 2 is 6.92 us long; three of seven are so, at 6.5 to 6.9, the others at 5.75 to 5.85. Half was taken, and about half came (in `x1_filler`, where the clock stays full, five of seven and 4.0 us). The Trainium skill's rule of the shared ports ("SBUF — State Buffer", section "SBUF: two separate sides"), which spoke against the change, agrees with this trace: the seven ada steps that run beside a GpSimd sum take 1.75 to 1.81 us instead of 0.75, while the 25 executions of Tm, inv and D beside one, which read a bank, keep their 0.67 to 0.69. The eight scalings at the start, one input and a constant, meet GpSimd too: 0.41 us at the median and up to 1.49. The same rule names such operations, where they run in a mode that reads through both ports, beside those with two inputs; the forecast had applied it to the latter alone.

```profile
L1790 DVE TENSOR_SCALAR XT<-XT x8: 411/412/1490, 50.2 to 55.7; 128x512 f32<-128x512 f32 x8
```

**The start came inside its bounds, the first head was missing.** The scalings, which the prediction didn't price at all, took 3.1 us more than before; what moving them gave is not clear of the noise (`x6_windows_xt`). In head 0 TE followed LD by 2.70 before and by 4.55 after, since S2, S1, S4 and the query stand there too; the sum counted six such places where there are seven.

**The signs.** The pitch of L1315, TE in levels 2 to 6, the longest tap (1.64), e_first (1.64) and TE of level 1 came as forecast, and L1315 waits for GpSimd only at the start of the stage (1.2 us in two places). "A head of about 54.1 us or less" did not: at full clock an inner head is 54.92.

**The step that failed** is "the 1.36 of the gate is eaten, +0.1 per head". It treats a wait of TensorE as worth its length. The prediction had read that the stage before runs at a granted clock of 1.00 [rows 2], with waits of at most 0.94 [rows 8], and took that rate for given when it put a later TE in their place, by the trace a wait of 2.12 us. The runs show it is not: the wait of 2.1 is followed by half the clock in five heads of seven (six of seven in `x9_after_pos`, the same stage), one of 1.10 in one head of six (`x5_windows`) and in none of twelve (`x6_windows_xt`, `x10_windows_xt_pos`). That was 10.5 us in the heads, more than the change's whole expected gain, and `x1_filler` gives 8.7 of it back with no other edit.

**The second miss** is that the sum ended at the stage's end. 8.1 us lie behind it. Of these 2.7 are tied to one load (3.6 in the medians); the rest falls together with stretches at half clock that are longer or more than before (nine behind the stage, 41 us together), and why they are isn't shown. No row of before could have told this size, but the range could have taken it in: before has seven such stretches behind the stage, 27 us together, and of the variants measured here the offset moved behind the stage by up to 9 us, nearly always upwards.

Of the rivals, the one that came nearest in time (2715, turns of GpSimd and VectorE) had its place wrong: levels 3 to 5 absorb their meetings, and the loss is at level 1. Without the fallen clock and the outside part the change would have stood at -2 us, inside the bound of no change.

## What to carry to other kernels

Price a new wait on the engine that sets the end by more than its length: look in the trace for waits of that length on that engine and read the granted clock behind them. Here a wait of 2.1 instead of 1.1 us cost its 1.0 and another 0 to 3.2 at half clock, 1.5 on the mean of seven heads.

An engine that is idle 90% of the time is not free to use. Before giving it work, list which instructions of VectorE run at each place, and put GpSimd's work beside those that read banks; here two waits on GpSimd were worth 20 us.

When code changes length, compare the two traces by their offset along the whole program, not by stage alone.

## What was not expected of the hardware

- Five useless matmuls in a wait made the kernel 9.3 us faster (2722.03 to 2712.76): TE still starts 5.33 us after LD, and no stretch at half clock is left in the heads.
- VectorE's one-input scaling of a tile in SBUF took up to 1.49 us beside GpSimd's sums instead of 0.41 to 0.42, more of a loss than any two-input operation had for its length.
- A load of 256 KB, issued at one place of the program, landed in 2.6 to 2.7 us in four of five kernels with the old stage (3.2 in `x8_delay11`) and in 3.5 to 3.7 in the five with the new one, 1.4 ms after the code that differs.
